# First mixer: the convolution of the last key channels stands one attention item later in VectorE's order

## The reference, cut to what matters

```python
qk = jax.nn.silu(_causal_dwconv(jnp.concatenate([q, k], -1), conv_w))
q, k = qk[..., :A_W], qk[..., A_W:]
```

```python
s = jnp.einsum('bqghd,bmgd->bqghm', qb, k_cmp)
p_cmp = _masked_softmax(s, ...)
o_cmp = jnp.einsum('bqghm,bmgd->bqghd', p_cmp.astype(dt), v_cmp)
...
o = gb[..., 0:1] * o_cmp + gb[..., 1:2] * o_sel + gb[..., 2:3] * o_win
```

## Time and profile before

| | |
|---|---|
| median of three runs | 3205.20 us |
| the profiled execution | 3205.01 us |
| its span on the core | 3203.5 us |
| TensorE busy | 3179.9 us (99%) |
| VectorE busy | 2020.7 us (63%) |
| ScalarE busy | 1419.3 us (44%) |
| GpSimd busy | 817.3 us (26%) |
| matmuls | 20113 |

### The profile page before, as it was taken

The page is one execution under the profiler, slowest core; times in us unless marked ns, Lnnn a source line. Parts: engine busy times, 40 slices in busy tenths (PEclk is TensorE's granted clock), DMA queues, the critical chain, the costliest instruction groups (busy, mean ns, idle before and its releaser), DMA issues.

```text
span 3203.5 us, 47455 instructions
## 1 busy us (share of the span) xinstructions
PE 3179.9 (99%) x20113; PEld 2850.5 (89%) x20116; DVE 2020.7 (63%) x2870; ACT 1419.3 (44%) x2146; POOL 817.3 (26%) x377
## 2 busy tenths in 40 slices
PE   8999999999999999999999999999999999999999
PEld 7887999988779999899998889999899998889998
DVE  6676755455857444586676637667667566466756
ACT  5355554443635444354353324435445433244533
POOL 1212033320510333202322130232123221312323
PEclk9999999999999999999999999999999999999999
DMA  5212233222103333324322332332333223223322
GB/s 177 83 40 73 80 106 119 99 99 73 66 27 112 106 115 104 112 67 125 112 91 90 110 99 67 122 116 87 99 99 126 85 93 108 90 92 99 121 91 79
DMA packets 223363, 308.95 MB, mean 96 GB/s; under 512 B 7888, under 2 KB 151264, under 8 KB 222896
## 3 DMA queue, kind: packets, MB, share of 16 engines
q1 hardware_dynamic: 219568, 291.41, 27.9%
q0 software_dynamic: 3584, 14.52, 1.3%
HBM read 303.80 MB, written 2.10 MB: 95 GB/s over the span
## 4 chain that ended last, share of the span: by engine, by line
PE 90%; DVE 7%; ACT 2%; DMA 1%; issue 0%; POOL 0%; SPq 0%; DVEq 0%; ACTq 0%
PE bank L610 27%; PE bank L612 27%; PE bank L611 27%; DVE wlo L2181 1%; PE bank L1037 1%; PE bank L634 1%; ACT whi L1379 1%; DMA wraw<-in_e_w_in 1%; DVE wkk_o L3065 1%; PE bank L1245 1%; DVE gb L3063 1%; PE bank L1320 1%; PE bank L1311 1%; PE bank L1023 0%; PE bank L1222 0%; PE bank L1223 0%
## 5 line engine op out<-in xcount | busy, mean ns | idle before, releaser
L3316 POOL TENSOR_TENSOR wlo<-wraw,whi 128x1024 fp32r<-128x1024 f32 (+1 forms) x173 | 455.2, 2637 | 1329.1 <-ACT whi L1379 1329.1
L610 PE MATMUL bank<-xh,whi 128*128 128x256 f32 (+1 forms) x2456 | 719.4, 293 | 10.3 <-DVE xl L2513 8.0
L1379 ACT ACTIVATE whi<-wraw 128x1024 fp32r<-128x1024 f32 (+2 forms) x399 | 435.3, 1096 | 629.8 <-PE bank L612 479.2
L611 PE MATMUL bank<-xl,whi 128*128 128x256 f32 (+1 forms) x2456 | 713.8, 291 | 0.0
L612 PE MATMUL bank<-xh,wlo 128*128 128x256 f32 (+1 forms) x2456 | 713.7, 291 | 0.0
L2181 DVE TENSOR_TENSOR wlo<-wraw,whi 128x1024 fp32r<-128x1024 f32 (+1 forms) x226 | 297.6, 1320 | 335.2 <-ACT whi L1379 334.2
L3316 POOL TENSOR_TENSOR wlo<-raw_w,whi 128x1024 fp32r<-128x1024 f32 x114 | 294.4, 2587 | 832.9 <-ACT whi L1379 832.9
L610 PEld LDWEIGHTS bank<-xh,whi 128*128 128x128 f32 x2456 | 464.1, 189 | 28.9 <-DVE wlo L2181 10.5
L610 PE MATMUL bank<-whi,uh_w 128*128 128x512 f32 (+1 forms) x1224 | 475.3, 388 | 0.0
L611 PE MATMUL bank<-wlo,uh_w 128*128 128x512 f32 (+1 forms) x1224 | 474.7, 388 | 0.0
L612 PE MATMUL bank<-whi,ul_w 128*128 128x512 f32 (+1 forms) x1224 | 474.7, 388 | 0.0
(11 more groups left out here) (411 smaller groups left out, 4948.9 us busy)
## 6 DMA issues: line engine op xcount, KB each, us to landing
wraw<-in_w_in SPq DMA_DIRECT2D x26, 1024.0 KB, 5.2
wraw<-in_ffn_w_gate SPq DMA_DIRECT2D x40, 512.0 KB, 4.9
raw_w<-in_ffn_w_gate SPq DMA_DIRECT2D x40, 512.0 KB, 4.9
raw_w<-in_ffn_w_up SPq DMA_DIRECT2D x40, 512.0 KB, 4.9
wraw<-in_ffn_w_up SPq DMA_DIRECT2D x40, 512.0 KB, 4.9
wraw<-in_ffn_w_down SPq DMA_DIRECT2D x20, 1024.0 KB, 5.0
raw_w<-in_ffn_w_down SPq DMA_DIRECT2D x20, 1024.0 KB, 5.1
raw_w<-in_mlp_w SPq DMA_DIRECT2D x19, 1024.0 KB, 5.0
```

What stands on the lines that cost most here:

```text
L610: M.matmul(o, lh, rh, start=start, stop=False, skip_group_check=more)
L611: M.matmul(o, lh, rl, start=False, stop=False, skip_group_check=more)
L1379: A.activation(hi, raw, ACT.Copy).then_inc(*k.w_hi.inc(("hi", j)))
L3316: G.tensor_tensor(lo[:, 0:n], raw[:, 0:n], hi[:, 0:n].bitcast(F), ALU.subtract).then_inc(*k.w_lo.inc(("lo", j)))
```

## The change

Only VectorE's program is touched, in the loop over the attention items. In round 1 VectorE no longer takes a unit, and in round 4 it takes two. So block 7's weight split, convolution and silu of block 6 stand in round 2 instead of round 1, behind the maxima of item 2 and the scaling of item 1. The silu of block 7 stands in round 3 instead of round 2, behind the maxima of item 3 and the scaling of item 2. From round 5 on the order is the old one.

```diff
             if 0 <= n - 1 < N:
                 scaled(n - 1)
-            next(units, None)
+            if n != 1:
+                next(units, None)
+            if n == 4:
+                next(units, None)
             if n >= 9 and n % 3 == 0:
                 next(units, None)
             if 0 <= n - 2 < N:
```

## The result

Before, 22 runs gave a median of 3205.23 us (3204.82 to 3206.25). With the change 22 runs gave 3210.49 us (3209.13 to 3211.91). The change costs 5.26 us, a ratio of 1.0016 with a 95% interval of 1.0010 to 1.0021. That is slower, but by less than the 0.2% that the prediction took as the bound of no change. The range forecast was 3205.6 to 3210.2 us: the result lies 0.3 us above its end. The likeliest case, 3207.8 us, was half as far from before as the result. The case that came about is the fourth rival, TensorE's clock (3209.9 us), which had a chance of 0.15.

The account below looks back on a forecast made before the run. The prediction took TensorE, busy 99% of the span, as the bound. A value product 2.65 us late, with the 0.96 us gain already counted, on 3205.01 us gave 3207.7, or 3207.8 us for the median; range 3205.6 to 3210.2 us.

Parts of the forecast that it names:

- the fourth rival: TensorE's clock falls in the gap before item 0's value product, +4.75 us in all, 3209.9 us; chance 0.15.
- Step 1: VectorE's scaling of item 1 would issue at 130.40 us, behind a reciprocal starting at about 130.21.
- Step 2: GpSimd's half of the weight split holds VectorE's scaling until 131.45; VectorE's next instruction starts at 131.71 us.
- Step 3: VectorE's weight split starts 2.72 us later; block 7's convolution starts at 132.85 and ends at about 135.95 us.
- Step 4: ScalarE's block 7 tanh and the queue behind it move by 2.72 us; copy of item 0 runs 137.48 to 137.84.
- Step 5: TensorE's value product of item 0 starts at 137.91, 2.65 us later; its gap grows from 0.96 to about 3.6 us.
- Step 6: From round 3 on, later work is covered by some 3 us or shifted alike on all engines.
- The sum: The value product's +2.65 us on the profiled execution's 3205.01 us, giving 3207.7 us; 3207.8 us for the runs' median.
- The other rival of the clock: TensorE's clock stays low for 8.4 us behind the gap, +6.85 us, 3212.0 us; chance 0.04.
- Only the lost wait counts: TensorE gains the 0.96 us because ScalarE's copy of item 0 does not hang on block 7's tanh: 3204.2 us; chance 0.07.
- GpSimd does not hold VectorE: Scaling of item 1 takes its usual 0.60 us, value product 1.94 us later, 3207.1 us; chance 0.08.
- Given back later: Part of the 2.65 us vanishes at TensorE's waits behind 136 us: 3205.2 to 3206.6 us; chance 0.09.

Follow-up runs that it names:

- Two experiments: Changed kernel with one weight tile's rest split by GpSimd alone, 3210.73 us, and by VectorE alone, 3210.71 us.
- the kernel with the gap filled: Changed kernel with TensorE making the second vo step's product twice, 24 unneeded matmuls more: 3207.50 us.
- two repeats: Kernel before, in its old order, with VectorE's first convolution instruction of block 7 done two more times: 3207.73 us.
- one repeat: Kernel before, in its old order, with VectorE's first convolution instruction of block 7 done once more: 3205.22 us.
- the copy first: Changed kernel with ScalarE's copy of item 0 at the start of round 2, ahead of block 7's tanh: 3209.56 us.

## Why the prediction was wrong, point by point

- **Step 1, the scaling issues at 130.40.** Right: 130.16 + 0.24 = 130.40.
- **Step 2, GpSimd holds it.** Right: GpSimd took 2.39 us (2.42 taken), and the split began at 131.44 + 0.24 = 131.68 (131.71). Two experiments confirm the cause.
- **Step 3, the convolution starts at 132.85.** Right: 132.57 + 0.24 = 132.81.
- **Step 4, ScalarE's copy of item 0 at 137.48.** Right: 137.19 + 0.24 = 137.43.
- **Step 5, the value product is 2.65 us late.** Right: 2.58 us, and the kernel with the gap filled cost 2.56 us. The split of the gap was not foreseen in size, but named: bank 0 first (2.02 us), then the copy (1.37 us).
- **Step 6, nothing is given back.** Right: the waits behind 150 us are the old ones.
- **The step that failed is what follows from the gap.** The sum treated 3.6 us of idle time as costing itself alone and left the clock to a rival of 0.15. The filled kernel shows what stood in its place: the wait cost 2.56 us and the fall of the clock another 2.70 us. The rival named three facts of the trace. Two are right: no wait behind the start was longer than 1.0 us, and after the one long idle time the matmuls ran at half the cadence (the profile's clock reads 1.00 in that stretch, so the cadence alone tells it). The first says nothing about a gap over three times as long. The third was misread. The granted clock was not "1.00 throughout": TensorE's last matmul ends at 3198.04, and the clock falls to half about 2.6 us later:

```profile
3198.00:3200.00 2.00, 0.04 (x1) 0.00 (x0) 1.46 (x5) 0.29 (x1) 0.00 (x0) 1.00 0.11 43
3200.00:3202.00 2.00, 0.00 (x0) 0.00 (x0) 0.79 (x2) 0.72 (x1) 0.00 (x0) 0.66 0.18 67
```

It costs nothing there, but it is the trace's own example of a fall in less idle time than the 3.6 us forecast. So both long idle times of the trace spoke for the fall, and so did the Trainium skill's page cited beside them. The likeliest case should have been the sum with the clock's price on it.
- **The price of the clock was mis-sized too.** It was taken as one number, 2.1 us, from one stretch at the start. The profile after lost 1.7 us and the median run 2.7 us. The spans on the core, which leave out what lies before and behind the work, go from 3207.8 to 3209.4 us in the 22 runs, against a median of 3206.2 us in the filled kernel: a price of 1.6 to 3.2 us. (The slowest time, 3211.91 us, has a span of 3209.4 us, so 2.5 us of it lie outside, where half of the 22 runs have 1.2 to 1.4.) With a spread up to 3.2 us instead of one number the range would have ended near 3211 and held the result. The other rival of the clock, a low clock over 8.4 us, did not come about, but the profile with two repeats comes near it: 0.60, 0.50, 0.50 and 0.70 in four stretches of 2 us make 0.80 + 1.00 + 1.00 + 0.60 = 3.4 us lost, some of it in idle time, from about 6.8 us at half.
- **The other rivals.** Only the lost wait counts: wrong, as forecast. GpSimd does not hold VectorE: wrong, as forecast. Given back later: wrong in the changed kernel.

The chance of 0.95 for no change beyond 0.2% stands: 5.3 us is 0.16%.

## What to carry to other kernels

When an engine's order is changed, follow what the moved instruction pushes back, not only what it pulls ahead: here a wait of 0.96 us was taken away, and the convolution, with another engine's queue behind it, came 2.7 us late. Do not let an engine in order stand at a wait while work that others need is queued behind it. If an estimate makes TensorE's gap longer than any gap in the trace over which the clock was seen to hold, look at the granted clock behind the trace's last matmul too, and price the clock into the likeliest case, as a spread and not as a number; filling such a gap with unneeded matmuls tells the clock's share from the waiting.

## What the runs showed of the hardware

- TensorE's clock held at 1.00 over a wait of 1.75 us (the profile of one repeat). It fell in the profiles with waits of 2.53 us, of 3.32 us, of 2.03 + 0.63 us and of 2.02 + 1.37 us with two transposes between. With 2.53 us and with 2.03 + 0.63 us both outcomes occur from run to run: three of eleven runs each have a mean granted clock of 1.000 and the short times, the other eight a lower one and the long times.
- The moment of the fall varies. With the copy first the clock fell about 1.9 us into the first wait, in the changed kernel only about 0.4 us after the value product had begun at 137.60, more than 4 us after the last dense matmul. Nor is the low stretch always the same: about 3.4 us in the changed kernel's profile, about 6.8 us in those of two repeats and of the copy first, part of which falls into idle time and costs nothing.
- The price varied from run to run of the same kernel: the changed kernel's spans go from 3207.8 to 3209.4 us, 1.6 us, where the filled one's spread over 0.7 us. The Trainium skill (TensorE: Matmul & The Clock Gate, Part 1) says that the clock is gated down after idle time and comes back with work, and the rows agree.
- More work can be faster: 24 unneeded matmuls (2.9 us) in the gap took 3.0 us off the changed kernel's time, 3210.49 to 3207.50 us in different sets of runs, or 2.7 us by each one's distance to before.
